# Three PSUM banks for turned probabilities, one bank for both mixers' sums, and FoX value pages sent ahead of selected values and raw rows

## The reference, cut to what matters

```
# NSA, per query block: three softmaxes over three sets of keys, summed with gates
oc  = softmax(q kc^T + bias) vc          # compressed keys, one per 16 rows
osl = softmax(q ks^T + bias, selected blocks) vs
ow  = softmax(q kw^T + bias, last 512 rows) vw
nsa = g0 * oc + g1 * osl + g2 * ow
# FoX: causal attention with a decay
l   = q k^T * scale + c_q - c_k          # c: running sum of log-forget
fox = softmax(l, causal) v
# both, for the prompt (blocks of 128 queries) and for the requests
# (their pages gathered by a page table)
```

## Time and profile before

| | |
|---|---|
| runs, median (lowest to highest) | 2829.06 us (2820.79 to 2832.17) |
| profiled execution, its own time | 2828.6 us |
| its span, first to last instruction | 2826.7 us |
| TensorE busy over the span | 2645.7 us (94%) |
| VectorE, ScalarE, GpSimd busy | 710.8, 548.9, 359.2 us |
| mean granted TensorE clock | 0.961 |

### The profile page before, as it was taken

The page is one execution under the profiler, slowest core; times in us unless marked ns, Lnnn a source line. Parts: engine busy times, 40 slices in busy tenths (PEclk is TensorE's granted clock), DMA queues, the critical chain, the costliest instruction groups (busy, mean ns, idle before and its releaser), DMA issues.

```text
span 2826.7 us, 29413 instructions
## 1 busy us (share of the span) xinstructions
PE 2645.7 (94%) x10923; PEld 1482.6 (52%) x10923; DVE 710.8 (25%) x1927; ACT 548.9 (19%) x1328; POOL 359.2 (13%) x573
## 2 busy tenths in 40 slices
PE   8998979889886688899999999999999999999999
PEld 4554654555554466656666445555555554444443
DVE  0000116656652244401111232222222220101222
ACT  0001016546541233300000121111111110010110
POOL 0000004434434000000000240000000000010110
PEclk9999988989987899899999999999999999999999
DMA  4115531011006667620112311111111114322400
GB/s 163 58 47 133 183 116 45 1 67 45 1 1 142 190 209 209 203 76 22 45 33 71 74 52 34 30 45 30 30 44 30 45 59 164 103 97 104 150 30 34
DMA packets 198343, 227.15 MB, mean 80 GB/s; under 512 B 52063, under 2 KB 149823, under 8 KB 196807
## 3 DMA queue, kind: packets, MB, share of 16 engines
q1 hardware_dynamic: 191418, 199.80, 23.6%
q0 software_dynamic: 5648, 16.33, 1.7%
q10 hardware_dynamic: 1168, 9.58, 1.0%
HBM read 203.60 MB, written 37.99 MB: 85 GB/s over the span
## 4 chain that ended last, share of the span: by engine, by line
PE 57%; ACT 0%; DVE 0%; issue 0%; DVEq 0%
PE ps L1953 23%; PE ps L2003 11%; PE ps L1903 8%; PE ps L2049 5%; PE ps L1906 4%; PE ps L1926 4%; PE ps L2007 1%; PE ps L1891 1%; PE ps L2052 0%; PE ps L1930 0%; PE ps L1960 0%; ACT arena L2139 0%; PE ps L1938 0%; PE ps L2033 0%; DVE arena L2261 0%; DVE qfT L2278 0%
## 5 line engine op out<-in xcount | busy, mean ns | idle before, releaser
L1953 PE MATMUL ps<-xT,qT 128*128 128x480 f32 (+1 forms) x2112 | 648.1, 469 | 0.0
L1953 PEld LDWEIGHTS ps<-xT,qT 128*128 128x128 f32 x2112 | 344.5, 191 | 296.4 <-issue 296.4
L2003 PE MATMUL ps<-arena 128*128 128x512 f32 x704 | 305.3, 593 | 0.0
L1903 PE MATMUL ps<-xT,arena 128*128 128x363 f32 (+1 forms) x768 | 244.5, 471 | 2.6 <-DVEq L2189 2.6
L2003 PEld LDWEIGHTS ps<-arena 128*128 128x128 f32 x704 | 132.6, 190 | 167.2 <-issue 166.7
L159 PE MATMUL ps<-w_rows,xT 128*128 128x512 f32 (+1 forms) x512 | 201.2, 551 | 5.0 <-DMA w_rows<-in_w_in 3.5
L1903 PEld LDWEIGHTS ps<-xT,arena 128*128 128x128 f32 x768 | 146.6, 191 | 92.5 <-DVEq L2189 2.8
L755 PE MATMUL ps<-ident,probs 128*128 128x128 f32 x816 | 140.5, 305 | 35.7 <-ACT xT L876 22.7
L867 ACT ACTIVATE probs<-probs,nmax 128x640 f32<-128x640 f32 (+7 forms) x192 | 142.6, 743 | 105.2 <-DVE nmax L829 58.5
L159 PEld LDWEIGHTS ps<-w_rows,xT 128*128 128x128 f32 x512 | 96.8, 192 | 99.1 <-issue 92.3
L2223 DVE TENSOR_SCALAR qfT<-qfT 128x480 f32<-128x480 f32 (+1 forms) x88 | 35.1, 420 | 443.9 <-ACT qfT L2098 443.9
(11 more groups left out here) (304 smaller groups left out, 2634.7 us busy)
## 6 DMA issues: line engine op xcount, KB each, us to landing
arena<-in_w_ffn_down SPq DMA_DIRECT2D x66, 512.0 KB, 3.5
arena<-in_cache_fox_kv SPq DMA_DIRECT2D x64, 256.0 KB, 5.4
xT<-in_cache_fox_kv SPq DMA_DIRECT2D x64, 256.0 KB, 6.3
arena<-in_cache_nsa_kv SPq DMA_DIRECT2D x64, 192.0 KB, 4.5
qT<-in_w_ffn_up SPq DMA_DIRECT2D x22, 512.0 KB, 4.0
qT<-in_w_ffn_gate SPq DMA_DIRECT2D x22, 512.0 KB, 5.2
bias_rows<-rev_dram ACTq DMA_DIRECT2D x8, 1160.0 KB, 20.1
arena<-in_w_in SPq DMA_DIRECT2D x16, 512.0 KB, 5.3
```

The costliest lines, as they stand in the source:

```text
L1903: pe.matmul(ps[:, 4 * (j % 2) + side, 0:n], at.w_gate[e][:, side, c, :], x[:, c, t0:t0 + n], start=(c == 0), stop=(c == KD - 1))
L1953: mm = pe.matmul(ps[:, 2 * (j % 3) + side, 0:n], at.w_ug[e][:, side, c, :], x[:, c, t0:t0 + n], start=(c == 0), stop=(c == KD - 1))
L2003: mm = pe.matmul(ps[:, q + h, :], hT[:, c, t0:t0 + m], at.w_down[:, load % RING, cols], start=(c == 0), stop=(c == NFF - 1))
```

## The change

In the prompt attention the turned halves go round three banks, 4, 5 and 7: chunk after chunk and half after half take the next. Half 0 then waits for VectorE's copies (`saved_b`) and half 1 for ScalarE's (`saved_a`), each counted for the half three before. Bank 6 holds the NSA sum in columns 0 to 255 and the FoX sum in columns 256 to 511, one place each; FoX values wait until the NSA sum of the same block is copied out, selected values until the FoX sum of the block before is. In the request attention, `window_and_values` is cut in two, and the pages 4 to 7 of FoX values are issued after the window, ahead of selected values, raw rows and the decay row.

```
--- before.py
+++ after.py
@@ -634,6 +634,14 @@
 FOX_SPLITS = [sum(q.branch == FOX and q.i > 0 for q in PAIRS[:n]) for n in range(NPAIR + 1)]
 
 
+TURN_BANKS = (4, 5, 7)
+
+
+def turn_bank(p, c, half):
+
+    return TURN_BANKS[(2 * (TURNED_BEFORE[p.n] + c) + half) % 3]
+
+
 def pair_no(turn, i, branch, j):
     return (turn * NTP + i) * 8 + ORDER.index((branch, j))
 
@@ -746,38 +754,37 @@
 
             def turn(p, c):
                 t0, m = p.chunks[c]
-                for half, turned, saved in ((0, turned_a, saved_a), (1, turned_b, saved_b)):
+                for half, turned, saved in ((0, turned_a, saved_b), (1, turned_b, saved_a)):
                     if c == 0:
                         pe.wait_ge(normed, 2 * p.n + half + 1)
-                    if TURNED_BEFORE[p.n] + c:
-                        pe.wait_ge(saved, TURNED_BEFORE[p.n] + c)
+                    if TURNED_BEFORE[p.n] + c + half >= 2:
+                        pe.wait_ge(saved, TURNED_BEFORE[p.n] + c + half - 1)
                     for x, (kt, s, w) in enumerate(p.tiles[t0:t0 + m]):
-                        mm = pe.transpose(ps[0:w, 4 + half, x * P:(x + 1) * P], probs_of(p, half, s, w), keep.ident[:])
+                        mm = pe.transpose(ps[0:w, turn_bank(p, c, half), x * P:(x + 1) * P], probs_of(p, half, s, w), keep.ident[:])
                     mm.then_inc(turned, 1)
 
             def weighted_values(p):
-                off, last = (p.i % 2) * 256, len(p.tiles) - 1
+                last = len(p.tiles) - 1
                 pe.wait_ge(saved_a, TURNED_BEFORE[p.n + 1])
                 pe.wait_ge(saved_b, TURNED_BEFORE[p.n + 1])
                 turned = turned_of(p)
                 done = NTP * p.turn + p.i
                 if p.branch == FOX:
-                    if done:
-                        pe.wait_ge(fox_saved, done)
+                    pe.wait_ge(nsa_saved, done + 1)
                     for j in range(2):
                         for x, (kt, s, w) in enumerate(p.tiles):
                             for half in range(2):
                                 h = 2 * (2 * p.turn + j) + half
-                                mm = pe.matmul(ps[half * HD:(half + 1) * HD, 7, off + j * P:off + (j + 1) * P],
+                                mm = pe.matmul(ps[half * HD:(half + 1) * HD, 6, 256 + j * P:256 + (j + 1) * P],
                                                keep.fv[:, kt, h * HD:(h + 1) * HD], turned[:, x, half, j, :],
                                                start=(x == 0), stop=(x == last))
                 else:
                     if p.branch == SLC and done:
-                        pe.wait_ge(nsa_saved, done)
+                        pe.wait_ge(fox_saved, done)
                     for x, (kt, s, w) in enumerate(p.tiles):
                         for half in range(2):
                             v = keep.vc[0:w, :] if p.branch == CMP else (keep.v_slc if p.branch == SLC else keep.v_win)[:, kt, :]
-                            mm = pe.matmul(ps[half * HD:(half + 1) * HD, 6, off:off + 256], v[:, half * HD:(half + 1) * HD],
+                            mm = pe.matmul(ps[half * HD:(half + 1) * HD, 6, 0:256], v[:, half * HD:(half + 1) * HD],
                                            turned[0:w, x, half].rearrange("p j q -> p (j q)"),
                                            start=(p.branch == SLC and x == 0), stop=(p.branch == WIN and x == last))
                 mm.then_inc(pv_done, 1)
@@ -843,7 +850,7 @@
                 if c == 0 and p.j == 0 and p.freed > 0:
                     dve.wait_ge(pv_done, p.freed)
                 nc.vector.tensor_copy(turned_of(p)[0:w, t0:t0 + m, 1, p.j, :],
-                                      ps[0:w, 5, 0:m * P].rearrange("p (t q) -> p t q", t=m)).then_inc(saved_b, 1)
+                                      ps[0:w, turn_bank(p, c, 1), 0:m * P].rearrange("p (t q) -> p t q", t=m)).then_inc(saved_b, 1)
 
             for p in PAIRS[0:AHEAD]:
                 logits(p)
@@ -874,16 +881,15 @@
                 if c == 0 and p.j == 0 and p.freed > 0:
                     act.wait_ge(pv_done, p.freed)
                 nc.scalar.copy(turned_of(p)[0:w, t0:t0 + m, 0, p.j, :],
-                               ps[0:w, 4, 0:m * P].rearrange("p (t q) -> p t q", t=m)).then_inc(saved_a, 1)
+                               ps[0:w, turn_bank(p, c, 0), 0:m * P].rearrange("p (t q) -> p t q", t=m)).then_inc(saved_a, 1)
 
             def save_out(p):
-                off = (p.i % 2) * 256
                 heads, cols = slice(2 * p.turn, 2 * p.turn + 2), slice(p.i * P, (p.i + 1) * P)
                 act.wait_ge(pv_done, p.group + 1)
                 if p.branch == WIN:
-                    nc.scalar.copy(keep.qT[:, heads, cols], ps[:, 6, off:off + 256].rearrange("p (j q) -> p j q", j=2)).then_inc(nsa_saved, 1)
+                    nc.scalar.copy(keep.qT[:, heads, cols], ps[:, 6, 0:256].rearrange("p (j q) -> p j q", j=2)).then_inc(nsa_saved, 1)
                 elif p.branch == FOX:
-                    nc.scalar.copy(keep.qfT[:, heads, cols], ps[:, 7, off:off + 256].rearrange("p (j q) -> p j q", j=2)).then_inc(fox_saved, 1)
+                    nc.scalar.copy(keep.qfT[:, heads, cols], ps[:, 6, 256:512].rearrange("p (j q) -> p j q", j=2)).then_inc(fox_saved, 1)
 
             for p in PAIRS[0:AHEAD]:
                 exps(p)
@@ -1197,11 +1203,13 @@
                     sp.wait_ge(fox_logits, 2 * n)
                 sp.dma_start(at.neg_c, io["neg_rows"][n * P:(n + 1) * P, :]).then_inc(neg_c_in, 16)
 
-            def window_and_values(n):
+            def window(n):
                 if n:
                     sp.wait_ge(nsa_pv, n)
                 for r in range(2):
                     sp.dma_start(at.win[:, r], io["state_nsa_win"][0, 2 * n + r].rearrange("(j p) k h d -> p j (k h d)", p=P)).then_inc(win_in, 16)
+
+            def selected_values(n):
                 for r in range(2):
                     for p in range(NPAGE):
                         sp.dma_start(at.v_slc[:, r, p, :], nsa_page(n, r, p)[:, 384:512]).then_inc(slc_v_in, 16)
@@ -1228,12 +1236,13 @@
                     page_ids(n + 1)
                     for p in range(4):
                         keys(n + 1, p)
-                window_and_values(n)
+                window(n)
+                for p in range(4, NPAGE):
+                    values(n, p)
+                selected_values(n)
                 if n + 1 < N_:
                     raw_rows(n + 1)
                     decay(n + 1)
-                for p in range(4, NPAGE):
-                    values(n, p)
             sp.wait_ge(ring_filled, ring.index[N_ - 1, "hidden1"] + 1)
             for e in range(2):
                 merge_weights(sp, ahead, io, m_there, e, slice(C_GA + e * P, C_GA + e * P + P),
```

10 lines of the change are left out of this document (5 added, 5 removed).

## The result

The changed kernel takes 2785.89 us (median of 4 runs, 2778.99 to 2789.85); before it was 2829.76 in the runs beside it. The ratio is 0.9848, with an interval of 0.9834 to 0.9862: 43 us faster. Run again among the experiments it had 0.9848 once more (0.9821 to 0.9874). The forecast was 2791, 38.5 us faster. The sum was nearly right, but its two parts were each wrong, by 11.6 and 8.7 us, in opposite directions.

What follows compares the result with a forecast made beforehand. TensorE's work plus its idle time bounds both attention stages. Gains of 15 + 17.4 + 6.1 = 38.5 us from 2828.6 give 2790.1, for the median 2791; own range 2784 to 2797, 8 in 10 within 2777 to 2808.

Steps and rivals of the forecast that it cites:

- part 1: Prompt attention, new banks: shorter waits of TensorE for copies of turned probabilities give 15 us, bounds 8 to 22.
- the 1.35: Prompt attention, block i=7: TensorE's 1.35 us wait for ScalarE's copy before 632.06 stays; only 0.1 us goes ahead.
- the gaps between selected and window pairs: Prompt attention, block i=7: waits of 0.28, 0.33 and 0.37 us around the first window pair; gain 1.1 us.
- the sign to look for: Prompt attention: waits for ScalarE's and VectorE's copies sum to about 20 us and not 38.
- the second rival: Prompt attention: GpSimd or the logits become late too, part 1 gives 2 and not 15: 2804 us; 13%.
- The clock of part 1: Prompt attention: no gain of TensorE's clock counted, as 1.2 us of the stall before the FoX values stay.
- The first rival: Prompt attention: TensorE's clock comes back too, 8.5 us more: 2782 us; 14%.
- The first wait of part 2: Request attention, first pair: value pages issued at 944.97, not 967.06, shorten TensorE's 22.1 us wait; gain 21.5 us.
- part 2: Request attention, SyncE's new order: 17.4 us at the first pair plus 6.1 at the next two; bounds 15 to 28.
- What is late next: Request attention, after the first pair: the decay row holds VectorE, then TensorE, 4.1 us; late keys beside it; net 17.4.
- Steps 1 and 2: Request attention, second and third pair: small waits for values go, gain 6.1 us; next keys just in time, no margin.
- The slower rival: Request attention: SyncE's issues take three times their 21 us, 84 us lost against 38 won: 2875 us; 3%.

Runs made afterwards that it cites:

- e4: Changed kernel, but in blocks 4 to 7 the first chunk of window pair 1 is turned twice (8 transposes more); ratio 0.9814.
- e3: Changed kernel with the decay row issued right behind the values, ahead of selected values and raw rows; ratio 0.9833.
- e2: Kernel before with only the new order of SyncE's queue, old banks; ratio 0.9932.
- e8: e7 with the doubled transposes of e4 added; 2754.53 us, ratio 0.9737.
- e9: Changed kernel, but at step 0 the FoX value pages go out ahead of the window; ratio 0.9861.
- e10: e8 with the edit of e9 (at step 0, FoX value pages ahead of the window); ratio 0.9736.
- e5: Changed kernel, but in blocks 4 to 7 ScalarE copies the first chunk of window pair 1 ahead of the exponentials of FoX pair 1; ratio 0.9798.
- e7: e5 plus another SyncE order: selected values behind step 1's keys or in the wait before values, decay row ahead of raw rows; 2761.44 us, ratio 0.9756.

## Why the prediction was right, and where it wasn't

**The idle time of part 1** had the right size, 15 forecast, 14 to 15 measured, by a path that was right in part. In the block of i=7 a wait for logits (1.03 us) took the place of VectorE's copy, the 1.96 stayed and the 1.35 is 1.10. But I was too careful with the gaps between selected and window pairs, which vanished wholly: waits for copies fell to 11.8 us, where "about 20 us" was the sign to look for. And I was too hopeful for the rest: waits for logits took back 6.0 us and those for GpSimd 3.5, the second rival at a part of its price. That both errors came to nothing in the sum was luck.

**The clock of part 1** was mis-sized. "As 1.2 us of that stall stay, I count no gain of clock" is the sentence that failed: the FoX values behind it went from 4.12 to 3.28 us at once, and the stage's busy time fell by 11.7 us on the mean. The first rival (8.5 us, 14%) came true beside the forecast, not in its place; it should have been a term of the sum. So part 1 gave 26.6 and not 15. By the Trainium skill (TensorE: Matmul & The Clock Gate, "A second HAM failure mode: psum-queue depth-cycling") frequent short idles cost throughput beyond their own length; the traces here agree: with 14.9 us of idle, 11.7 of busy time went.

**The first wait of part 2** was mis-sized: 21.5 forecast, 17.1 measured from the start of the hidden layer to the end of the values (41.4 to 24.3 us; 23.8 when run again). The step that failed is the place in time of the queue. I took 944.97 from the old list, 7.4 us after the hidden layer began; SyncE issued the pages 10.5 us after it (9.4 when run again). Where it was early, in e4 (5.4 us after), the values ended 19.1 us after the hidden layer's start, near the forecast's 19.9, and the first pair of requests gained 15.2 us, though the whole stage was no shorter than in the others (322.0). Besides, the first page came 8.6 us after its issue, where I had the last land 6.3 to 7.9 after its own, and the matmuls behind the wait ran at half speed for a part (5.22 us for 16, which take 3.65 elsewhere). I had named that last one and left it out. The wait itself, about 5 us forecast and 5.2 measured, agrees by chance: I had it spread over the pages, and it stands whole before the first.

**What is late next** was half right. The place and size were (4.1 us forecast, 5.2 measured), the cause wasn't: "the decay row" with "keys ... beside it and not on top". It is the keys; with the decay row first, VectorE's wait is gone and TensorE waits for the keys as before (e3). And the rows behind this stall, 2.0 us dearer at the lower clock, were left out too, so step 0 to 1 gave 10.3 us and not 17.4.

**Steps 1 and 2**: the waits for values went, 6.1 us; "just in time" for the next keys was too tight. New waits for keys took 2.8 and 1.7 us of it, and 1.9 to 4.8 us were left in the two traces. In all the order gave 14.8 us (339.8 to a mean of 325.0 over the changed kernel, its repeat, e2, e4 and e5) and not 23.5.

**The sum**: 26.6 + 14.8 = 41.4 by the traces, 43 by the runs, 38.5 forecast. Two errors cancelled, 11.6 us too little in part 1 and 8.7 too much in part 2; that the total came so near was luck. The first is the clock. Of the second, the clock behind the two stalls of step 0 is 3.6 us (1.6 and 2.0), and the later start of the queue 3.1. The slower rival had nothing for it: the queue's issues kept their pace behind the new wait, 9.16 and 11.38 us at step 1.

## What to carry to other kernels

Where an engine that waits in many short stalls is also the one with a clock, count the clock on both sides: here each microsecond of idle taken away by the banks gave, on the mean, 0.8 more in faster matmuls, and repeating cheap transposes in a stall that can't be shortened paid too (e8). In an in-order queue, put a wait only ahead of what may be late; work that is ready belongs in front of it, and the item to check is the first one behind, the next step's keys. And a repair that moves one wait often shows in the next one (e9: a wait of 4 us gone at the values, 3 us more at the keys), so test it where that next one has been taken away. Where two lists run side by side, take the place of one against the other from more than one trace: the start of SyncE's list against the hidden layer lies within 5.7 us over the eleven traces with the new order, and differs by 1.2 us between two executions of the same kernel.

## What the runs showed of the hardware that I had not expected

One program's clock is not one number: with the same idle time (46.3 to 47.6 us) six executions had TensorE busy for 379 to 388 us in the prompt attention, and lengths in two groups 7 us apart. Short stalls are followed by slow rows: behind stalls of 1.96 and 1.10 us with one transpose between them, eight transposes took 1.97 us in all six, against 1.09 at full speed, and 1.19 where the first stall was half filled (e4). And work can be free: with 64 transposes more, TensorE was busy for 378.2 and 379.4 us (e8, e10), without them for 378.5 and 378.6 (e5, e7).
